# Laying a tile's products over the half-levels of a gated recurrence, with two value banks in turn and one shared bank for turned keys and turned outputs

## The reference, cut to what matters

```python
def _hgrn2_chunk(S0, xs):
    """Exact chunkwise form of S_t = diag(f_t) S_{t-1} + k_t v_t^T, o_t = S_t^T q_t."""
    ...
    att = jnp.einsum('bthk,btshk,bshk->bhts', q, decay, k)
    o = (jnp.einsum('bhts,bshv->bthv', att, v)
         + jnp.einsum('bthk,bhkv->bthv', q * jnp.exp(G), S0))
    ...
    S = (jnp.exp(G_end)[..., None] * S0
         + jnp.einsum('bshk,bshv->bhkv', k * jnp.exp(G_end[:, None] - G), v))
```

## Time and profile before

| | us |
|---|---|
| median of 3 runs (lowest, highest) | 2984.74 (2979.95, 2987.5) |
| the profiled execution, its own time | 2986.96 |
| its span in the profile | 2985.1 |
| round 0 of the recurrence, 723.5 to 753.1 | 29.6 |
| round 1, to 792.3 | 39.2 |
| round 2, to 824.2 | 31.9 |
| the tail, to 842.5 | 18.3 |
| mean granted clock of TensorE over the span | 0.981 |

### The profile page before, as it was taken

One profiled execution on the slowest core, in us unless ns is written; L12 is line 12 of the kernel. 1 busy time (PEld: TensorE's weight loads), 2 busy tenths in 40 slices (PEclk: granted clock), 3 DMA queues, 4 the chain that ended last, 5 costly groups with the idle time before them and its releaser, 6 DMA issues. The chain is left out here.

```text
span 2985.1 us, 61072 instructions
## 1 busy us (share of the span) xinstructions
PE 2845.5 (95%) x24985; PEld 2643.7 (89%) x24985; DVE 1745.8 (58%) x3140; ACT 1007.2 (34%) x2102; POOL 1535.0 (51%) x1377
## 2 busy tenths in 40 slices
PE   6999999997789999999999999999999999999998
PEld 5859999765689999999999999956699999999998
DVE  6399999556656743445797500066648543346785
ACT  3351111355433433333232301165525333333232
POOL 2121224464533777776577232144424777776675
PEclk8999999998899999999999999999999999999999
DMA  6716763652241122224222223163221212224322
GB/s 220 255 63 227 252 222 122 175 180 75 92 172 56 56 82 86 74 77 152 81 86 86 77 91 114 44 218 113 68 88 50 86 65 87 80 72 137 123 69 69
DMA packets 192053, 338.85 MB, mean 114 GB/s; under 512 B 27784, under 2 KB 107424, under 8 KB 189920
## 3 DMA queue, kind: packets, MB, share of 16 engines
q1 hardware_dynamic: 138832, 266.50, 26.8%
q10 hardware_dynamic: 52944, 68.45, 6.6%
HBM read 268.30 MB, written 79.49 MB: 117 GB/s over the span
## 5 line engine op out<-in xcount | busy, mean ns | idle before, releaser
L740 POOL TENSOR_TENSOR ah_ring_lo<-ah_raw,ah_ring_hi 128x512 fp32r<-128x512 f32 (+2 forms) x426 | 579.7, 1369 | 237.0 <-ACT ah_ring_hi L1149 146.5
L109 PE MATMUL tr_acc<-tr_quad_hi,ah_ring_hi 128*128 128x264 f32 x2432 | 693.5, 285 | 7.7 <-ACT tr_kept L1160 2.6
L111 PE MATMUL tr_acc<-tr_quad_hi,ah_ring_lo 128*128 128x264 f32 x2432 | 692.0, 285 | 0.0
L110 PE MATMUL tr_acc<-tr_quad_lo,ah_ring_hi 128*128 128x264 f32 x2432 | 689.6, 284 | 0.0
L109 PEld LDWEIGHTS tr_acc<-tr_quad_hi,ah_ring_hi 128*128 128x128 f32 x2432 | 457.9, 188 | 9.4 <-ACT tr_kept L1160 3.0
L110 PEld LDWEIGHTS tr_acc<-tr_quad_lo,ah_ring_hi 128*128 128x128 f32 x2432 | 458.0, 188 | 0.1
L111 PEld LDWEIGHTS tr_acc<-tr_quad_hi,ah_ring_lo 128*128 128x128 f32 x2432 | 457.5, 188 | 0.0
L2917 DVE CUSTOM_DVE_ANT_0 pc_prob<-pc_dots,pc_bias 128x640 f32<-128x640 f32 (+4 forms) x128 | 79.1, 655 | 283.6 <-POOL pc_bias L2720 261.7
L1779 DVE TENSOR_SCALAR_CACHE_REDUCE f_q<-score,choose_trial 128x384 bf16<-128x384 f32 (+6 forms) x224 | 242.2, 1145 | 1.1
L2083 POOL CAST f_w_hi<-f_raw 128x512 fp32r<-128x512 f32 x66 | 46.2, 700 | 375.2 <-DMA f_raw<-in_w_dram 203.8
L738 POOL CAST ah_ring_hi<-ah_raw 128x512 fp32r<-128x512 f32 (+1 forms) x114 | 72.3, 634 | 277.7 <-PE tr_acc L111 257.1
(11 more groups left out here) (410 smaller groups left out, 7430.6 us busy)
## 6 DMA issues: line engine op xcount, KB each, us to landing
f_ada_w<-in_w_ada_dram SPq DMA_DIRECT2D x48, 1024.0 KB, 5.6
scratch_inner<-tr_kept ACTq DMA_DIRECT2D x88, 264.0 KB, 2.4
ah_raw<-in_w_gate_dram SPq DMA_DIRECT2D x44, 512.0 KB, 3.5
ah_raw<-in_w_up_dram SPq DMA_DIRECT2D x44, 512.0 KB, 4.5
ah_raw<-in_w_down_dram SPq DMA_DIRECT2D x64, 256.0 KB, 3.1
f_raw<-in_w_dram SPq DMA_DIRECT2D x24, 512.0 KB, 7.4
out_z_dram<-f_stage ACTq DMA_DIRECT2D x60, 176.0 KB, 1.9
out_z_dram<-tr_value ACTq DMA_DIRECT2D x48, 176.0 KB, 1.9
```

The lines of the kernel that those rows point to most:

```text
L109: pe.matmul(out, w_hi, hi, start=start, stop=False, skip_group_check=onto)
L110: pe.matmul(out, w_hi, lo, start=False, stop=False, skip_group_check=onto)
L111: return pe.matmul(out, w_lo, hi, start=False, stop=stop, skip_group_check=onto)
L740: pool.tensor_tensor(lo[:, 0:width], own, hi[:, 0:width].bitcast(F32), ALU.subtract).then_inc(w_ready, 1)
```

## The change

- **Products.** `updates` moves from half-level 1 to 0 of a tile's four. `values` is split: heads 0 and 1 stay in half-level 1, heads 2 and 3 go to half-level 2. The keys of a round's first tile are turned before the round's first `pairs`, and those of the other two one half-level earlier than before (3 and 7).
- **VectorE.** `state_update`, `inverse_roots` go one half-level later (3, 5), `finish` one earlier (6). `LAST` is 15 and not 16.
- **Banks.** `out` has two banks in turn. For this, turned keys and turned outputs share one, `flip`: `turn_keys` now also waits for `finish` of an earlier tile, and `turn_out` for `turned_keys`.
- **ScalarE.** `gate_silus` runs Silu ahead of round 1's loop and takes one square root of a dummy, `root_first`. The gate's scaling goes in twos at half-levels 0 and 5. In `place_late` VectorE keeps the four copies for tile 6 and ScalarE takes the four for tiles 7 and 8.

```diff
-    LAST = 2 * LEVELS + 2
+    LAST = 2 * LEVELS + 1
...
-        kT_ps, dS, out, turn = (m.ps(f"hg_{x}_ps", [P, 512]) for x in ("kT", "dS", "out", "turn"))
+        flip, dS = (m.ps(f"hg_{x}_ps", [P, 512]) for x in ("flip", "dS"))
+        out = [m.ps(f"hg_out{b}_ps", [P, 512]) for b in range(2)]
...
             if name == "kT":
                 eng.wait_ge(kT_copied, before + 1)
+                turned = min(p - 2, LAST_AHEAD) if p % 3 else p - 1
+                if turned >= 0:
+                    eng.wait_ge(finished, turned + 1)
             elif name == "dS":
                 eng.wait_ge(state_ready, HB * (before + 1))
             elif name == "out":
-                eng.wait_ge(o_scaled, HB * (before + 1))
+                if p >= 2:
+                    eng.wait_ge(o_scaled, HB * (p - 1))
             else:
                 eng.wait_ge(finished, before + 1)
+                eng.wait_ge(kT_copied, TILES + 1 if p >= 3 * (ROUNDS - 1) else min(p + 2, p - p % 3 + 3))
...
-                    for t in tiles_at(n - 1, at, 2):
+                    for t in tiles_at(n - 1, at, 3):
                         state_update(t)
-                    for t in tiles_at(n - 1, at, 4):
+                    for t in tiles_at(n - 1, at, 5):
                         inverse_roots(t)
-                    for t in tiles_at(n - 1, at, 7):
+                    for t in tiles_at(n - 1, at, 6):
                         finish(t)
...
+            def gate_silus():
+                act.wait_ge(own.gate_in, 16)
+                act.activation(gate[:], gate[:], ACT.Silu).then_inc(gate_silu, 1)
+                act.wait_ge(eps_set, 1)
+                act.activation(root_first[:], eps[:], ACT.Sqrt)
+
...
             for n in range(ROUNDS):
+                if n == 1:
+                    gate_silus()
                 for at in range(LAST):
-                    for t in tiles_at(n - 1, at, 0):
-                        turned_keys(t)
-                    if n == 1 and at < HB:
-                        gate_scale(at)
+                    if at >= 3:
+                        for t in tiles_at(n - 1, at, -1):
+                            turned_keys(t)
                     for t in tiles_at(n - 1, at, 3):
                         squares(t)
                     for t in tiles_at(n - 1, at, 5):
                         scaled(t)
+                    if n == 1 and at in (0, 5):
+                        for hd in (range(HB // 2) if at == 0 else range(HB // 2, HB)):
+                            gate_scale(hd)
                 place(n)
+                if n + 1 < ROUNDS:
+                    turned_keys(3 * n)
...
             for n in range(ROUNDS):
+                if n:
+                    turn_keys(3 * (n - 1))
                 for pr in range(2):
                     pairs(n, 0, pr)
...
+                    if at >= 3:
+                        for t in tiles_at(n - 1, at, -1):
+                            turn_keys(t)
                     for t in tiles_at(n - 1, at, 0):
-                        turn_keys(t)
+                        updates(t)
                     for t in tiles_at(n - 1, at, 1):
-                        updates(t)
-                        values(t)
+                        values(t, first_heads)
+                    for t in tiles_at(n - 1, at, 2):
+                        values(t, last_heads)
```

More of the change, by code:

```diff
@@ L3325, in recurrence @@
         SWAPPED = TILES - 1
+        LAST_AHEAD = 3 * (ROUNDS - 1) - 1
         def bank(name, p):
-            main, spare = {"kT": (kT_ps, ring[0][0]), "out": (out, ring[0][1]), "dS": (dS, ring[1][0]), "turn": (turn, ring[1][1])}[name]
+            main, spare = {"kT": (flip, ring[0][0]), "out": (out[p % 2], ring[0][1]), "dS": (dS, ring[1][0]), "turn": (flip, ring[1][1])}[name]
             if name == "out" and p == TILES:
@@ L3347, in bank_free @@
             if before < 0:
+                if name == "turn":
+                    eng.wait_ge(kT_copied, 2)
                 return
@@ L3467, in place_late @@
                 dve.wait_ge(masked, masked_no(n, SMALL, 1))
[L3468 to L3472, removed]
+                for b in range(4):
+                    own_rows = slice(32 * b, 32 * b + 32)
+                    dve.tensor_copy(att[n % 2][own_rows, :, 32 * b:32 * b + 32].rearrange("p (h j) m -> p h j m", j=3)[:, :, 0],
+                                    near[n % 2][own_rows].rearrange("p (h j) m -> p h j m", j=3)[:, :, 0]).then_inc(placed_late, 1)
             for n in range(ROUNDS):
@@ L3544, in _ @@
                 silus(n)
+            def gate_silus():
[3 more added lines that the diff above has]
+                act.activation(root_first[:], eps[:], ACT.Sqrt)
             def gate_scale(hd):
[L3547 to L3550, removed]
+                act.wait_ge(gate_silu, 1)
                 act.activation(gate[:, hd, :], gate[:, hd, :], ACT.Copy, scale=head.gnorm[:, hd:hd + 1]).then_inc(gate_done, 1)
             act.wait_ge(att_zero, 2)
-            act.wait_ge(eps_set, 1)
             def place(n):
@@ L3614, in _, with place_late @@
                         scaled(t)
+                    if n == 1 and at in (0, 5):
+                        for hd in (range(HB // 2) if at == 0 else range(HB // 2, HB)):
+                            gate_scale(hd)
                 place(n)
+                if n + 1 < ROUNDS:
+                    turned_keys(3 * n)
+            def place_late():
+                n = ROUNDS - 1
+                act.wait_ge(masked, masked_no(n, SMALL, 1))
+                for b in range(4):
+                    own_rows = slice(32 * b, 32 * b + 32)
+                    act.activation(att[n % 2][own_rows, :, 32 * b:32 * b + 32].rearrange("p (h j) m -> p h j m", j=3)[:, :, 1:3],
+                                   near[n % 2][own_rows].rearrange("p (h j) m -> p h j m", j=3)[:, :, 1:3], ACT.Copy
+                                   ).then_inc(placed_near, 1)
             turned_keys(TILES - 2)
             turned_keys(TILES - 1)
+            place_late()
             squares(TILES - 2)
@@ L3687, in updates, with values @@
                 last.then_inc(dS_done, 1)
-            def values(p):
+            def values(p, heads):
                 t = tile_at[p]
@@ L3709, in values @@
                 bank_free(pe, "out", p)
-                for hd in range(HB):
+                for hd in heads:
                     own_out = bank("out", p)[:, P * hd:P * hd + P]
@@ L3713, in values @@
                     last = pe.matmul(own_out, r[:, hd, P * t:P * t + P], state[s][:, hd, :], start=False, stop=True)
-                last.then_inc(out_done, 1)
+                if heads[-1] == HB - 1:
+                    last.then_inc(out_done, 1)
             def turn_out(p):
@@ L3740, in _ @@
             updates(TILES - 1)
-            values(TILES - 2)
+            values(TILES - 2, range(HB))
             turn_keys(TILES)
-            values(TILES - 1)
-            values(TILES)
+            values(TILES - 1, range(HB))
+            values(TILES, range(HB))
             updates(TILES)
```

4 lines of the change are left out of this document (3 added, 1 removed).

## The result

| | before | after |
|---|---|---|
| median (lowest, highest), 22 runs of each | 2987.26 (2979.23, 2992.26) | 2992.48 (2983.79, 2997.53) |
| the profiled execution, its own time | 2986.96 | 2988.5 |

The ratio is 1.002, with a 95% interval of 1.0012 to 1.0027. The change loses some 0.2%, where 0.3 to 0.4% less was forecast, and the range of 2967 to 2983 did not hold it.

What follows compares the result with a forecast made beforehand. The stage was taken as a chain of waits with no engine full. Gains of 7.4 (round 1), 4.1 (round 2) and 0.3 (tail) less 0.8 (turn) gave 11.0 us, forecast 2975 us, range 2971 to 2978, 8 in 10 2967 to 2983.

Steps and rivals of the forecast that it cites:

- The inverse root now stands behind the last `rise`, which costs 0.5 of it: End of round 2, from `pairs` 8 to the last `turn_out`: 10.3 us walked against 12.1, gain 1.8 despite this 0.5.
- The walk: The new order of the stage stepped through with the old trace's durations; round 1 25.9 us, round 2 gaining 4.1.
- the missing 11.2 us: Over round 1, turn, round 2 and tail, 73.4 us was predicted against 84.5 before; 84.6 was measured.
- rival A: Waits only move: each of six cycles in the rounds 0.8 us longer, for example; gain 2 to 9 us, chance 0.30.
- Its own sign of being wrong: TensorE's clock at 0.5 over more than 8 us after 760 was named as one sign against the forecast.
- ScalarE frees the keys in time: Round 1: two scalings done 5.8 us after its start, TensorE has the second tile's keys turned at 6.8.
- the dummy root: ScalarE's one-column activation before round 1: priced at 0.3 us, between 0 and 0.30, and covered by slack.
- The new waits: `turn_keys` waiting for `finish`: about 0.8 us at round 2's first, over 1 us at round 1's third, walked as 1.6.
- The turn: From round 1's last `turn_out` to round 2's start: 3.2 us against 2.4, a loss of 0.8.
- The tail: After round 2: the 1.1 us gap before `values` of tile 7 goes, gain 0.3; 17.6 us predicted against 17.9.
- the case without a gain: Whole kernel: no gain or a loss under 9 us, chance 0.06.
- C: TensorE's clock stays at 1.2 GHz through both rounds: up to 26 us more, 15 net, 2990; chance 0.03.

## Why the prediction was wrong

**"The inverse root now stands behind the last `rise`, which costs 0.5 of it" is the step that failed.** I priced one `rise` and forgot what else the change had put on VectorE between the last tile's squares and its root: the third tile's state update, also a half-level later, 1.11 us, and GpSimd's work beside the two `rise`, which made them 2.31 us together, 1.15 each, where I took 0.55 to 0.9. In round 1 the complement is 0.63 us of that, as the run without it shows; in round 2 the pair took 2.10. In place of 0.5 us the stop grew by 2.3 in round 1 and 2.1 in round 2. Moving the root back and the state update behind the last `rise` brought it to 1.19 us and the time from 1.0005 (0.9994 to 1.0015) to 0.9981 (0.997 to 0.9992) on one chip: this is shown, though the intervals only just part, and 0.9981 is half of the forecast gain. On the next chip the same two moves with a third one gave 0.9992 (0.9983 to 1.0001).

**The second part of it is what the stop triggers.** The walk kept the slow clock of before and added none. Of the missing 11.2 us, in the traces of before and after:

- stops beyond the 0.5 us each: (3.74 - 1.42 - 0.5) + (3.52 - 1.42 - 0.5) = 3.4 us
- the clock: 9.41 - 3.80 = 5.6 us more of TensorE's busy time at the lower level around the turn, and 1.3 more in the tail (4.86, where before 3.52 of the first 3.6 us were at 0.57). At the full clock such work takes 0.44 less (a tile's `updates` 1.16 against 2.08), so 2.5 + 0.6 = 3.1 us
- stops marked "issue" in rounds 1 and 2: 0.91 + 0.57 + 0.89 + 0.92 = 3.3 us against 0.22 + 1.56 = 1.8, so 1.5
- `updates` waiting for the state update before it: 0.58 + 0.57 = 1.2 us. The walk let tile 4's `updates` run from 0.65 to 1.85 beside tile 3's state update, 0.8 to 1.9, though both use the one `dS` bank. In the second trace of the changed kernel round 1 has two such waits, 1.82 and 0.94 us
- the remaining 2.0 us, not told apart: the clock was low until about 762 and not 760 in round 1, and the walk gave each cycle no slack (rival A's argument)

These are estimates from single rows, and not all of each need lie on the path. The kernel with the long stops filled shows that the clock follows such a stop, and its stretch is 3.6 us shorter, near the 3.1. But two traces of one kernel differ by more, and neither filled kernel's time stands apart from its unfilled neighbour's, so the clock's price is an estimate that no time confirms. What an "issue" stop costs the median is not shown either.

**Its own sign of being wrong** was a clock at 0.5 over more than 8 us after 760, and it came: 13.2 us around the turn and 6.5 in the tail.

**What held.** ScalarE frees the keys in time, the table load cost 1.28 us with the root 1.29 us behind its start, and the dummy root 0.20 where 0.3 was taken. The first scalings end at 766.06, 7.5 us after round 1's start and not 5.8, for the late DMA, and this was covered by TensorE's late `turn_keys`. `values` no longer waits. The new waits stand where they were put: 0.88 us at the first `turn_keys` of round 2 and 1.16 at the third of round 1, where 1.6 was walked. The second is not steady: 0.68 in the other trace of the same kernel, and 0.32 in the three with the root moved and the scalings left in place.

**The turn** cost 4.3 us and not 3.2, as its transposes (1.09 against 0.6) and its `pairs` ran at the lower level. **The tail** lost 0.8 for the same reason: the copies shared with ScalarE did their part, but it began at clock 0.50.

**The rivals.** What came is the case without a gain, to which I gave 0.06 with no mechanism behind it. A, that waits only move, came nearest by its mechanism, but had its lower end at a gain of 2 us. C asked for a low clock through both rounds, and that did not come: 0.99 from 799.2 to 823.7. Its sum is also off: 26 us less the 11 is a loss of 15, which is 3000 and not 2990. But a lower clock did come at another place. The Trainium skill ("TensorE: Matmul & The Clock Gate", section "A second HAM failure mode: psum-queue depth-cycling") ties the clock's swings to frequent short idles between groups of matmuls. The traces do not agree for the waits within a round (the clock is 0.99 from 799.2 to 823.7, over 0.89, 0.92 and 0.93). What they show is a fall behind one long stop, of 3.74 or 3.52 us at a round's end. I had weighed it over the rounds, and not at the one stop that my own change lengthened.

**What stays open.** The traced pair has equal stretches, 85.2 each, while the ratio was 1.002 in one comparison and 1.0005 in the other. Between two profiled executions of the changed kernel the stretch varied by 4.4 us, and round 0, whose code order no run changed, took 25.4 to 31.8 us. There the length goes with the "issue" stops: where round 0 took 25.4 to 26.5 us, they sum to 0.7 to 2.2 us, and where it took 28.4 to 31.8, to 4.4 to 6.3. The change's 5 us in the medians can't be given a row. Part of it may be such stops; which part was not separated.

## What to carry to other kernels

When a step is moved behind others on an engine, list everything that stands between its input and it, also what the same change has moved there, and price each at what it takes beside the engine that runs then. Look also for the one bank that two steps share when you move them towards each other. At the end of a loop nothing covers a delay: there the late step stops TensorE, and in the traces TensorE's clock fell behind a stop of 3.7 us and made the work after it slower as well. Put first on the queue what another engine waits for (the root), and last what only the next round needs (the state). Filling a stop with unused work held the clock in one trace, and won no time that the runs show.

## What the runs showed of the hardware

- **Instruction stops at fixed places.** TensorE stood 0.2 to 3.8 us with no releaser, at places of the instruction stream 124 to 127 matmul records apart, the same places in seven traces of six kernels. 32 records more ahead moved the stops by 32 records in the work, so that their count from the start stayed the same. Their length varies from trace to trace: 2.06 us and 1.37 at the same 62 records of the changed kernel and of the one with the root moved, and 2.89 in front of 49 records of round 0 in the first where the second has none. Behind the longest, 3.82 us, the granted clock was 0.50 for 4.5 us.
- **Long and short stops and the clock.** Behind 3.74 us the granted clock was at 0.50 until 799.2; with 22 unused transposes in that stop it stayed at 1.00. Short stops do not decide it by themselves. With root and state update moved, TensorE was busy 2.85 of 5.9 us to the end of round 1, with stops of 0.93, 1.19 and 0.93 us, and the level then fell to 0.50 for 3.3 us. With the keys behind the `pairs` the third of these is 0.29, and it stays at 1.00. At the end of round 2 both kernels have 0.93, 1.19 and 0.93; behind them the clock is 0.63 from 815.4 to 820.0 in the first and 1.00 from 815 to 822 in the second.
- **GpSimd beside VectorE.** A 128x384 multiplication takes 0.54 us alone on VectorE, and two take 2.31 beside GpSimd's keys and complement. The Trainium skill ("SBUF — State Buffer", section "Who interferes with whom") says that a VectorE instruction with two SBUF inputs and a GpSimd instruction that reads SBUF keep each other out; the trace agrees in direction. GpSimd's two complements took 2.23 us beside it and 1.63 alone. Which of the two is slowed goes with which starts first: in the changed kernel GpSimd's multiplication starts 0.03 us before the `rise` and takes 0.83 us, and with root and state update moved it starts 0.05 us behind one and takes 1.20, while that `rise` takes 0.56.
